# Products without a reader in TensorE's waits for norms, gates and experts, in a four-layer fp32 block

## What is computed

```python
def modulate(x, shift, scale):
    return rms_norm(x) * (1 + scale) + shift
...
    for l in range(DEPTH):                     # first block
        a_lat = modulate(h_lat, sh_a, sc_a)    # and a_ctx
        o_lat = mixer(a_lat, a_ctx) ...        # attention
        h_lat = h_lat + g_a * o_lat
        h_lat = h_lat + g_f * swiglu(modulate(h_lat, sh_f, sc_f), ffn_w_gate_up[l], ffn_w_down[l])
    x = rms_norm(h_lat, final_norm)
    for l in range(DEPTH):                     # second block
        proj = rmsnorm(x, norm_mix[l]) @ w_in[l]
        ...                                    # pool, conv + layernorm, two attentions, short conv
        x = x + cat @ w_out[l]
        x = x + peer_ffn(rmsnorm(x, norm_ffn[l]), peer_wq[l], peer_subkeys[l], peer_u[l], peer_v[l])
...
def peer_ffn(xn, wq, subkeys, u_tab, v_tab):
    sc = (xn @ wq) . subkeys                   # key scores
    idx, g = top-16 of the sums of two top-16 lists, softmax   # 8 heads
    act = gelu(einsum('ckd,cd->ck', u_tab[ic], xc))
    return einsum('ck,ckd->cd', gc * act, v_tab[ic])
```

## Time and profile before

| | us |
|---|---|
| median of 3 runs | 3377.08 (3373.78 to 3378.36) |
| profiled execution, its own time | 3372.12 |
| its span, first to last instruction | 3370.6 |
| TensorE busy | 3150.4 (93%), 18836 records |
| VectorE busy | 1972.9 (59%) |
| ScalarE busy | 1586.5 (47%) |
| GpSimd busy | 274.8 (8%) |

### The profile page before, as it was taken

How to read it: one execution, slowest core, us unless ns; L and a number is a source line. 1 busy time by engine, 2 the same in 40 slices (tenths; PEclk the granted TensorE clock), 3 DMA queues, 4 the chain that set the end, 5 groups by cost and what they waited for, 6 DMA issues and landing times.

```text
span 3370.6 us, 49973 instructions
## 1 busy us (share of the span) xinstructions
PE 3150.4 (93%) x18836; PEld 2673.9 (79%) x18836; DVE 1972.9 (59%) x4121; ACT 1586.5 (47%) x3320; POOL 274.8 (8%) x376
## 2 busy tenths in 40 slices
PE   6998999998899978997999999998899789999999
PEld 3745677776699867986789999988788678999998
DVE  3233433335666556689666666656659876666665
ACT  2254322223655425319555555542541765555554
POOL 0021000000200021008000000001200620000000
PEclk9999999998999988999999999999799999999999
DMA  6502444432155423440455556543144035555554
GB/s 227 178 1 76 156 175 161 166 105 94 45 170 180 156 73 103 152 144 1 157 187 187 186 185 200 182 162 110 56 162 152 30 113 182 187 188 187 184 186 150
DMA packets 135052, 479.82 MB, mean 142 GB/s; under 512 B 15520, under 2 KB 17440, under 8 KB 134048
## 3 DMA queue, kind: packets, MB, share of 16 engines
q1 hardware_dynamic: 132944, 471.26, 42.6%
q10 hardware_dynamic: 1872, 5.38, 0.4%
HBM read 475.53 MB, written 1.05 MB: 141 GB/s over the span
## 4 chain that ended last, share of the span: by engine, by line
PE 88%; DVE 5%; ACT 3%; issue 2%; DMA 1%; POOL 0%; SPq 0%; DVEq 0%; ACTq 0%; POOLq 0%
PE psum L768 15%; PE psum L770 15%; PE psum L769 15%; PE psum L2941 7%; PE psum L2943 7%; PE psum L2942 7%; PE psum L2850 7%; PE psum L2759 4%; PE psum L863 2%; PE psum L1125 2%; PE psum L356 1%; PE psum L1135 1%; PE psum L629 1%; DMA raw<-in_mod_w 1%; DVE a_scaled L733 1%
## 5 line engine op out<-in xcount | busy, mean ns | idle before, releaser
L249 DVE TENSOR_TENSOR w_lo<-raw,w_hi 128x512 fp32r<-128x512 f32 x1424 | 958.4, 691 | 744.9 <-ACT w_hi L240 717.6
L240 ACT ACTIVATE w_hi<-raw 128x512 fp32r<-128x512 f32 x1424 | 864.4, 625 | 795.7 <-PE psum L770 419.3
L768 PE MATMUL psum<-x_hi,w_hi 128*128 128x256 f32 x1968 | 561.2, 285 | 7.7 <-issue 4.2
L770 PE MATMUL psum<-x_hi,w_lo 128*128 128x256 f32 x1968 | 558.2, 284 | 0.0
L769 PE MATMUL psum<-x_lo,w_hi 128*128 128x256 f32 x1968 | 557.7, 283 | 0.0
L2941 PE MATMUL psum<-w_hi,wt_hi 128*128 128x512 f32 x1024 | 406.9, 397 | 6.5 <-DVE wt_lo L3005 6.5
L2943 PE MATMUL psum<-w_hi,wt_lo 128*128 128x512 f32 x1024 | 406.4, 397 | 0.0
L2942 PE MATMUL psum<-w_lo,wt_hi 128*128 128x512 f32 x1024 | 405.8, 396 | 0.0
L768 PEld LDWEIGHTS psum<-x_hi,w_hi 128*128 128x128 f32 x1968 | 373.5, 190 | 17.6 <-issue 9.0
L769 PEld LDWEIGHTS psum<-x_lo,w_hi 128*128 128x128 f32 x1968 | 376.1, 191 | 7.9
L770 PEld LDWEIGHTS psum<-x_hi,w_lo 128*128 128x128 f32 x1968 | 375.1, 191 | 0.0
(11 more groups left out here) (336 smaller groups left out, 4439.0 us busy)
## 6 DMA issues: line engine op xcount, KB each, us to landing
raw<-in_v SPq DMA_DIRECT2D x256, 512.0 KB, 4.4
raw<-in_u SPq DMA_DIRECT2D x190, 512.0 KB, 3.4
raw<-in_mod_w SPq DMA_DIRECT2D x96, 512.0 KB, 4.4
raw<-in_w_gate_up SPq DMA_DIRECT2D x88, 512.0 KB, 5.2
u_raw<-in_u SPq DMA_DIRECT2D x66, 512.0 KB, 3.5
raw<-in_w_in SPq DMA_DIRECT2D x40, 512.0 KB, 3.5
raw<-in_w_down SPq DMA_DIRECT2D x32, 512.0 KB, 3.5
raw<-in_w_peer SPq DMA_DIRECT2D x32, 512.0 KB, 4.2
```

What stands on the lines that cost most here:

```text
L240: self.nc.scalar.activation(self.hi[:, m % 4, :], self.half(m), ACT.Copy).then_inc(self.rounded[m % 4], 1)
L249: self.nc.vector.tensor_tensor(self.lo[:, m % 4, :], self.half(m), self.hi[:, m % 4, :], ALU.subtract).then_inc(self.ready[m % 4], 1)
L768: pe.matmul(out[:, 0:width], hi[:, w], x_hi, start=(c == 0), stop=False)
L770: mm = pe.matmul(out[:, 0:width], lo[:, w], x_hi, start=False, stop=(c == total - 1))
```

## The change

Seven, fourteen or twenty products of the identity with itself (128 by 128, fp32) are put on TensorE's queue at 20 places, 257 in all. Each writes the first 128 columns of the bank that the next real product fills, with `start=True`, so nothing of them is left. They stand before the semaphore wait for the data, but behind the wait for the bank. For that the bank's wait is moved ahead of the data's in the norms' spread, in the gates and in `add_up`; neither wait is dropped.

```diff
+SPARE = 14
...
+    def turn_over(self, out, n):
+
+        for _ in range(n):
+            self.nc.tensor.matmul(out[:, 0:P], self.ident, self.ident, start=True, stop=True)
...
     def tensor_spread(self):
         k, pe, starts = self.k, self.k.nc.tensor, self.starts()
         for s, (use, j, _, dst) in enumerate(self.inv):
-            pe.wait_ge(*self.spread.after(s + 1))
             if j == 0:
                 pe.wait_ge(*use.free())
+            if s == 0 and len(self.inv) == 1:
+                k.turn_over(dst, SPARE // 2)
+            pe.wait_ge(*self.spread.after(s + 1))
...
-def product(k, out, cuts, x, width, arrive=None):
+def product(k, out, cuts, x, width, arrive=None, spare=0):
+
 
     pe = k.nc.tensor
+    k.turn_over(out, spare)
     c, total = 0, sum(cuts)
...
             pe.wait_ge(*use.free())
-            product(k, use.tensor, self.cuts, self.x, self.width, self.arrive if n == 0 else None)
+            product(k, use.tensor, self.cuts, self.x, self.width, self.arrive if n == 0 else None,
+                    SPARE if n == 0 and self.arrive is not None else 0)
...
-                product(k, use.tensor, [DC], a, self.width, arrive)
+                product(k, use.tensor, [DC], a, self.width, arrive, SPARE if arrive is not None else 0)
...
         for g, use in enumerate(self.uses):
+            pe.wait_ge(*use.free())
+            if g == 0:
+                self.k.turn_over(use.tensor, SPARE)
             pe.wait_ge(*self.numbers.emptied(g + 1))
             pe.wait_ge(*self.scaled.after(g + 1))
             pe.wait_ge(*self.by_pool.after(g + 1))
-            pe.wait_ge(*use.free())
...
-        pe.wait_ge(*self.lo.after(t + 1))
         if t == 0:
             for a in self.acc:
                 pe.wait_ge(*a.free())
+            k.turn_over(self.acc[0].tensor, SPARE + 6)
+        pe.wait_ge(*self.lo.after(t + 1))
```

## The result

The changed kernel takes 3397.59 us (median of 6 runs, 3395.19 to 3404.28) where the kernel before took 3377.72 beside it: ratio 1.0065, 95% interval [1.0052, 1.0078]. It is slower, by about 20 us where 8 were forecast, and 1.6 us above the range. The profiled execution's span is 3394.9 us, 24.3 more than before.

A forecast was written before the change was run, and what follows sets the result against it. The prediction took TensorE, 88% of the chain that ended last, to bound the kernel, except where it waits. Its place-by-place terms summed to +8.0 us on a 3377.1 us median, giving 3385.1 us, with a range of 3374 to 3396.

The forecast's parts named there:

- +1.5 each: Gates, two layers: fillers make the first product 1.5 to 3.1 us late, partly regained; +1.5 us each, +3.0 together.
- the experts came out as forecast: Experts, two layers: 20 fillers overrun the idle time before the first accumulation; +1.1 us each, +2.2 together.
- first norm: Start of the kernel: no idle at the spread products, so seven fillers purely delay a serial chain; +2.5 us.
- FFN norm, layer 0: Spread at 362.92: seven fillers overrun 0.70 us of idle, slow at first and turning fast midway; +1.2 us.
- attention norm, layer 1: Spread at 781.38: faster spread and a later half-clock stretch sped up outweigh a small overrun; -1.0 us.
- FFN norm, layer 1: Idle of 1.59 us exactly holds seven fillers, and the last step is no longer slow; -0.3 us.
- final norm: First block, spread at 1134.49: no idle, clock full, seven fillers are pure delay on the chain; +1.6 us.
- mixer norm, layer 0: Spread at 1143.39: overrun of 0.7 us, regained by faster spread and plain products; -0.3 us.
- rival C: Everywhere: fillers run slow and don't raise or hold the clock in time; +20.6 us, 3398 us; chance 0.12.
- Rival A: Clock held everywhere, decided at the mixer attention's norm (1250.54), where attention behind must speed up; -7 us, 3370; chance 0.17.
- Rival B: Overruns at the start, final norm and gates are absorbed by unseen slack; +0.9 us, 3378 us; chance 0.13.
- The rule weighed: Whole kernel: half of the throttled 229 us can be won, up to 115 us, so the change should be clearly faster.

The follow-up runs named there:

- the old order: The changed kernel with all its fillers, but the gates' waits in their order of before from group 1 on; ratio 1.0048 to the kernel before.
- the first kernel: The kernel before with only the gates' bank wait moved ahead of the three waits for data, no fillers; ratio 1.0025 to the kernel before.
- norms and products alone: The changed kernel without its parts at gates and experts: 7 fillers at the norms' spreads, 14 at the first plain products; ratio 1.0029 to the kernel before.
- norms alone: The changed kernel with only the 7 fillers ahead of the norms' spread products, gates' and experts' waits as before; ratio 1.0024 to the kernel before.

## Why the prediction was wrong

**The step that failed** is the one on the gates, "+1.5 each", and in it a term that was left out. Of the diff's move of the bank's wait ahead of the three others, the sum held only what it lets group 0 do. For the other 63 groups the forecast had no term at all, since the four waits are the same four. It measured 5.3 and 4.9 us by itself and, with the experts' fillers running slow behind the longer loop, routing to accumulation came to +8.0 and +7.8 in the two layers, against the 2.6 a layer forecast for gates and experts together. The third wait's place is what makes it dear: S moved from the second semaphore instruction ahead of the weight load to the first. With the old order it is +1.3 to +2.3. There the experts came out as forecast, +1.0 against +1.1. The gates did not: the forecast had the first product 1.5 to 3.1 late and gave back 0.9. It came 1.6 or 1.7 late (2.6 once), and the loop behind it was 1.3 to 1.5 us shorter. So +0.2 to +0.3 was left in three of the four layers measured (two kernels) and +1.3 in one, not +1.5. The order of waits by itself is 10.2 us (the first kernel, both layers) of the 24.3. In the changed kernel against the one with the old order it is 15.8 - 2.6 = 13.2 us, both layers' routing to accumulation, which takes in that the experts' fillers began at half clock, though the forecast took the dense gate products ahead of them as a reason that they wouldn't. That they did so because of the longer loop is argued, not shown.

**The norms were mis-sized.** Term by term, forecast and then the four traces that have these fillers (the changed kernel, with the old order, norms and products alone, norms alone), each over the stretch from the norm's sums of squares to the place named, or else to the next norm's sums:

| place | forecast | traces |
|---|---|---|
| first norm (to its spread at 40.78) | +2.5 | +2.6, 2.0, 3.0, 2.9 |
| FFN norm, layer 0 | +1.2 | +1.2, 2.4, 2.8, 3.6 |
| attention norm, layer 1 | -1.0 | +1.7, 4.2, 1.8, 4.3 |
| FFN norm, layer 1 (to 982) | -0.3 | -0.3, -0.3, -0.3, 0.0 |
| final norm (at 1134.49) | +1.6 | +1.6, 1.6, 1.6, 1.6 |
| mixer norm, layer 0 (to 1222) | -0.3 | +1.5, 4.2, 1.5, 2.2 |
| norm before routing, layer 0 (to the turned results) | -0.3 | +0.3, 0.3, 0.3, 1.5 |
| mixer norm, layer 1 (to 2334) | less than in layer 0 | +0.6, 0.7, 0.6, 1.2 |
| norm before routing, layer 1 (to the turned results) | -0.3 | +0.3, 0.3, 1.8, 1.5 |

Where both semaphores were up or the clock was full, the price from the rows held. The FFN norm of layer 1 was met as well. Elsewhere, where I let fillers "hold the clock", they didn't: they came behind the norms' one-column sums, ran at half clock themselves, and the clock fell again behind them or rose too late for the spread. That is rival C's mechanism, and its 3398 is close to the 3397.6 measured. But it was right at these norms and not at the gates, where it had put 6.2; its sum came out close by chance. In kernels without these fillers the attention norm's stretch moved between -1.6 and +1.9 from trace to trace, and the mixer norms' between -0.6 and +4.1. So a gain of 1.0 at the attention norm is not what the fillers brought, but whether they cost 2 or 4 there, and what they cost at the mixer norms, the traces don't settle.

**The rest.** Rival A fell at its own deciding point: with seven fillers at 1252.60 TensorE still idled 3.96, and the attention behind ran at 0.51. Even with 24 there the clock was held only to 1254, and no more than 1.7 us came of it, in one layer. Rival B fell with VectorE's wait for the first weighing, 2.27 after against 1.80. I had it at 3.3: the first product came 1.6 late as forecast, but the products of the first groups then ran at full clock. The rule weighed (half of the throttled time can be won) was rightly set aside: the time at the lower level fell from 229 us to (1 - 0.972) x 2 x 3394.9 = 190, and the kernel is slower, though the moved waits have their part in that. Counted from the last group's product, the first accumulation came 4.2 us later (1629.08 - 1620.47 = 8.61, before 4.40), where 2.7 was forecast; with the old order it was 2.6.

## What to carry to other kernels

A wait is not only a condition but also has a place: in a loop paced by a hand-over between two engines, see in the trace on which instruction the wait that comes last has landed. Here it was cheapest written first, on the weight load itself, and dearest on the instruction furthest ahead, since the others still had to be gone through after it. Treat a reordering of waits as an edit that is paid in every round. Fillers paid here only where they fit in the idle time, behind work that is dense already, and ahead of a stretch that TensorE itself paces; at the norms most of them cost time. When an edit has a part for one iteration and a part for all, price the part for all first.

## What the runs showed of the hardware

- The time from the end of ScalarE's scaling to the start of the product that waits for it was 0.05, 0.10, 0.14 or 0.25 us, with that wait written first, second, fourth or third of four. The records show it on the weight load in the first case, on the semaphore instruction just ahead of the load in the next two, and on the one ahead of that in the last. The weights are not loaded early in the quick cases: the load stands 0 to 0.03 us ahead of the product in all of them.
- A filler of 128 columns in fp32 took 0.235 us (20 in 4.70) at full clock and up to 0.47 (7 in 3.27) at half. 20 that began at half clock took 6.33, with a granted clock of 0.57 over 1623 to 1627 and 1.00 behind.
- The same instructions up to layer 0's FFN norm (358.73 before), unchanged in ten of these kernels, ended from 5.3 us earlier to 5.3 us later in single profiled executions; so a term of a microsecond has to be read between neighbouring rows, not from the span.
